# One PSUM input for the wide operations of a top-sixteen selection

## The reference, cut to what matters

```
q = (hf @ w_q).reshape(t, 8, 2, 64)
sc = einsum('thcd,hcnd->thcn', q, sub_keys)         # 2 x 128 scores a head and token
sv, si = top_k(sc, 16)
cand_s = (sv[:, :, 0, :, None] + sv[:, :, 1, None, :]).reshape(t, 8, 256)
cand_i = (si[:, :, 0, :, None] * 128 + si[:, :, 1, None, :]).reshape(t, 8, 256)
fs, fp = top_k(cand_s, 16)
eidx = take_along_axis(cand_i, fp, axis=-1)
gates = softmax(fs, axis=-1)
act = gelu(x . u_emb[eidx]);  out = sum over chosen of gates * act * v_emb[eidx]
```

## Time and profile before

| | us |
|---|---|
| median of 3 runs | 990.34 (989.86 to 990.83) |
| profiled run | 990.89 |
| its span | 989.0 |
| TensorE busy | 925.8 (94%) |
| VectorE busy | 734.6 (74%) |
| ScalarE busy | 529.0 (53%) |
| GpSimd busy | 464.1 (47%) |

### The profile page before, as it was taken

One profiled execution on the slowest core, in us unless ns is written; L12 is line 12 of the kernel. 1 busy time (PEld: TensorE's weight loads), 2 busy tenths in 40 slices (PEclk: granted clock), 3 DMA queues, 4 the chain that ended last, 5 costly groups with the idle time before them and its releaser, 6 DMA issues.

```text
span 989.0 us, 20056 instructions
## 1 busy us (share of the span) xinstructions
PE 925.8 (94%) x5888; PEld 828.0 (84%) x5888; DVE 734.6 (74%) x1591; ACT 529.0 (53%) x1042; POOL 464.1 (47%) x370
## 2 busy tenths in 40 slices
PE   7679399999979889999999999999999999999998
PEld 7546168899979889999999999988888888888886
DVE  5999944203999930388888888688888888888886
ACT  7333075555544445555555555665556666566653
POOL 4668406587999998877777777500000000000000
PEclk8789799999999999999999999999999999999999
DMA  9424022315556556656556556677767767776773
GB/s 341 155 86 155 16 85 75 118 55 202 197 186 210 183 199 215 210 198 202 196 189 205 191 190 202 202 252 237 250 237 243 241 237 245 235 245 238 246 240 134
DMA packets 67436, 191.39 MB, mean 194 GB/s; under 512 B 6480, under 2 KB 8272, under 8 KB 67408
## 3 DMA queue, kind: packets, MB, share of 16 engines
q1 hardware_dynamic: 67408, 191.04, 57.0%
HBM read 173.71 MB, written 17.30 MB: 193 GB/s over the span
## 4 chain that ended last, share of the span: by engine, by line
PE 66%; POOL 11%; DVE 10%; issue 8%; ACT 3%; DMA 1%; POOLq 0%; SPq 0%; DVEq 0%; ACTq 0%
PE ps L423 21%; PE ps L425 20%; PE ps L424 20%; POOL w_lo L1462 10%; DVE routing L731 4%; PE ps L660 3%; DVE routing L876 2%; DVE small L731 1%; PE ps L405 1%; DVE route_t L731 1%; DMA routing<-in_w_in 1%; DVE raw L731 1%; ACT w_hi L1168 1%; ACT h_hi L1175 0%; POOL w_lo L1426 0%
## 5 line engine op out<-in xcount | busy, mean ns | idle before, releaser
L1462 POOL TENSOR_TENSOR w_lo<-raw,w_hi 128x512 fp32r<-128x512 f32 x256 | 345.6, 1372 | 79.2 <-ACT w_hi L1318 78.8
L1318 ACT ACTIVATE w_hi<-raw 128x512 fp32r<-128x512 f32 x512 | 308.3, 628 | 132.2 <-PE ps L425 131.3
L423 PE MATMUL ps<-h_hi,w_hi 128*128 128x256 f32 x1088 | 309.6, 285 | 16.5 <-POOL w_lo L1462 15.2
L424 PE MATMUL ps<-h_lo,w_hi 128*128 128x256 f32 x1088 | 307.8, 283 | 0.0
L425 PE MATMUL ps<-h_hi,w_lo 128*128 128x256 f32 x1088 | 307.8, 283 | 0.0
L423 PEld LDWEIGHTS ps<-h_hi,w_hi 128*128 128x128 f32 x1088 | 208.7, 192 | 19.4 <-POOL w_lo L1462 17.4
L731 DVE TENSOR_TENSOR w_lo<-raw,w_hi 128x512 fp32r<-128x512 f32 x256 | 177.4, 693 | 52.5 <-ACT w_hi L1318 41.1
L424 PEld LDWEIGHTS ps<-h_lo,w_hi 128*128 128x128 f32 x1088 | 208.8, 192 | 0.0
L425 PEld LDWEIGHTS ps<-h_hi,w_lo 128*128 128x128 f32 x1088 | 208.8, 192 | 0.0
L423 PE MATMUL ps<-w_hi,hot_gate 128*128 128x512 f32 x512 | 199.2, 389 | 0.0
L424 PE MATMUL ps<-w_lo,hot_gate 128*128 128x512 f32 x512 | 199.2, 389 | 0.0
(11 more groups left out here) (195 smaller groups left out, 914.9 us busy)
## 6 DMA issues: line engine op xcount, KB each, us to landing
raw<-in_u_t SPq DMA_DIRECT2D x128, 512.0 KB, 3.3
raw<-in_v SPq DMA_DIRECT2D x128, 512.0 KB, 3.3
act_spill<-acts SPq DMA_DIRECT2D x62, 256.0 KB, 2.1
acts<-act_spill SPq DMA_DIRECT2D x62, 256.0 KB, 3.4
routing<-in_w_in SPq DMA_DIRECT2D x5, 2048.0 KB, 11.4
routing<-in_w_out SPq DMA_DIRECT2D x2, 2048.0 KB, 8.4
routing<-in_w_q SPq DMA_DIRECT2D x2, 2048.0 KB, 8.0
xs<-in_x SPq DMA_DIRECT2D x2, 512.0 KB, 4.0
```

What stands on the lines that cost most here:

```text
L423: pe.matmul(dst, s_hi, m_hi, start=first and i == 0, stop=False)
L424: pe.matmul(dst, s_hi, m_lo, start=False, stop=False)
L1318: A.activation(w_hi[:, 2 * (s % 2) + h, :], raw[:, s, h * HALF:(h + 1) * HALF], ACT.Copy)\
L1462: G.tensor_tensor(w_lo[:, slot, :], raw[:, s, h * HALF:(h + 1) * HALF], w_hi[:, slot, :].bitcast(F32), ALU.subtract).then_inc(lo_ready, 1)
```

## The change

Each of the wide operations with two inputs gets one of them from PSUM. The pair sum reads the second set's best values from best_p (bank 3), into which a new copy puts them. The compare reads iota_p (bank 2) in place of iota, and writes its result to match_p (banks 4 to 7) in place of w2; the product reads match_p. For this the iota copy and its two waits stand ahead of the selection instead of ahead of the one-hots, and a wait for all eight score copies (sc_ready at 8) stands ahead of the compares. Operation counts: two copies more, everything else as before. No engine but VectorE has a changed instruction.

```
+        best_p = ps[:, 3, 0:PH * PK].rearrange("p (h k) -> p h k", h=PH)
+        match_p = ps[:, 4:8, :].rearrange("p b n -> p (b n)").rearrange("p (h a b) -> p h a b", h=PH, a=PK)
...
-            iota_k = iota[:, 0:PK].unsqueeze(1).unsqueeze(1).to_broadcast(shape)
+            iota_k = iota_p[:, 0:PK].unsqueeze(1).unsqueeze(1).to_broadcast(shape)
+            dve.wait_ge(pq_ready, PH)
+            V.tensor_copy(iota_p, iota).then_inc(iota_ready, 1)
+            dve.wait_ge(iota_ready, 1)
             for t in range(TT):
                 dve.wait_ge(sc_ready, 4 * t + 4)
                 best([top[:, c, h, :] for c, h in ch_rows], [idx[:, c, h, :] for c, h in ch_rows],
                      [sc[:, t, c, h, :] for c, h in ch_rows], [work[:, c, h, :] for c, h in ch_rows])
                 did(V.tensor_copy(idx_f, idx))
-                step(tt(w2, top[:, 0].unsqueeze(3).to_broadcast(shape), top[:, 1].unsqueeze(2).to_broadcast(shape), ALU.add))
+                step(V.tensor_copy(best_p, top[:, 1]))
+                step(tt(w2, top[:, 0].unsqueeze(3).to_broadcast(shape), best_p.unsqueeze(2).to_broadcast(shape), ALU.add))
...
                 step(V.tensor_copy(ab_f, ab))
+                dve.wait_ge(sc_ready, 8)
                 for c in range(2):
-                    step(tt(w2, ab_f[:, c].unsqueeze(3).to_broadcast(shape), iota_k, ALU.is_equal))
-                    step(tt(w3, w2, idx_f[:, c].unsqueeze(2).to_broadcast(shape), ALU.mult))
+                    step(tt(match_p, ab_f[:, c].unsqueeze(3).to_broadcast(shape), iota_k, ALU.is_equal))
+                    step(tt(w3, match_p, idx_f[:, c].unsqueeze(2).to_broadcast(shape), ALU.mult))
...
-            dve.wait_ge(pq_ready, PH)
-            V.tensor_copy(iota_p, iota).then_inc(iota_ready, 1)
-            dve.wait_ge(iota_ready, 1)
             one_hots(0, first=True)
```

## The result

| | kernel before | changed kernel |
|---|---|---|
| median, us (runs) | 990.23 (4) | 974.19 (4) |
| lowest to highest | 989.86 to 990.83 | 973.15 to 975.58 |
| span of the profiled run | 989.0 | 971.9 |
| ratio, 95% interval | | 0.984 (0.982 to 0.986) |

The changed kernel is 16.0 us faster; 973.9 had been forecast, with a range of 972.6 to 977.0.

The account below looks back on a forecast made before the run. The prediction took TensorE to be held in the selection by GpSimd subtractions, which VectorE's wide operations with two SBUF inputs slow. Median 990.34 - 16.62 (loss) + 0.2 (small operations) = 973.9 us, range 972.6 to 977.0.

Parts of the forecast that it names:

- The size, 16.62 us: Key stage beside the selection: 28 tiles took 97.26 us instead of 80.64; the change gives back all 16.62 us.
- The ruler: ScalarE's gelu, one per tile of the key stage, used to size the loss: 2.88 us a tile when nothing is late.
- the view of waits: Profile view in which TensorE waited ten times, 14.0 us, always for the GpSimd subtraction w_lo.
- part 1: Selection's ten operations take one input from PSUM: GpSimd keeps its own pace, 2.55 us a tile, giving back 16.62 us.
- VectorE at 2.28 us an operation: Selection's ten 2048-element operations: 22.8 us instead of 32.0, 9.2 us less on VectorE, worth nothing by itself.
- parts 2, 3: Two best_p copies, 0.6 us on VectorE, hidden by idle time; iota copy moved ahead of the selection, costed at nothing.
- part 5: Selection's four compares write PSUM: between 0 and 9.7 us more on VectorE, taken as 0, either end inside idle time.
- part 6: Small SBUF operations of the selection still hold GpSimd: 0.2 us taken, bounds 0 and 2.7 us.
- The wait for the exponentials: VectorE's wait for ScalarE's exponentials after the selection: about 24 instead of 32.49 us.
- Partial release: Rival, chance 0.06: compares writing PSUM still hold GpSimd, sums and products let it go; 979.9 us.
- no release: Rival, chance 0.03: long instructions, not a second SBUF input, hold GpSimd; time stays at 990.3 us.
- Slower: Rival, chance 0.01: dear PSUM accesses make VectorE's selection late for ScalarE's exponentials; about 998 us at 7 us each.

Follow-up runs that it names:

- e3: Only the compares read PSUM (iota_p), and they write SBUF; sums and products read two SBUF tensors; 983.33 us, ratio 0.993 to the kernel before.

## Why the prediction was right

- *What bounds the stage.* Right. GpSimd set the pace beside the ten operations, in eight tiles of the selection (two of them held two operations each and lost 3.3 us), and TensorE in the tiles between; the changed kernel has all tiles at 2.88.
- *The size, 16.62 us.* Measured 16.61 between the first gelu and the exponentials. The ruler served better than the view of waits (14.0): it is what TensorE's work cost, without modelled ends.
- *GpSimd is let go by one PSUM input* (part 1). Right, and the step that carried the forecast. The rows for it were from another stage, with other forms and lengths; the separate kernels show it for sums, compares and products alone. The Trainium skill's rule in "SBUF — State Buffer", "Who interferes with whom", agrees in all of them: two SBUF inputs hold GpSimd (1.3 to 1.9 us of TensorE's time each), one doesn't, if the instruction is outside the two-port modes. Which mode the shift and the casts ran in that still waited with one input, no run here shows.
- *VectorE at 2.28 us an operation*: 2.29 to 2.30. The surcharge for a PSUM source that the Trainium skill has in "VectorE: DVE Perf Modes", section on the TRN2 errata (62 cycles, as an estimate 65 ns), didn't show: 2288 ns for the sums with a PSUM operand against 2286 for a reduce from SBUF and 2.28 us for a sum with both inputs in SBUF.
- *The copies* (parts 2, 3): 0.28 us each for best_p, 0.29 for iota_p, hidden by VectorE's idle time. Both waits were met. Without the reads they moved nothing.
- *Writing PSUM* (part 5): 2296 ns for a compare, 10 more than for the same compare with its output in SBUF (e3, 2286), as the 11 ns worked out for the copy had it. The low end of the bounds was the right one.
- *The small operations* (part 6) were the one term that I had taken above zero, 0.2 us. They lengthened a subtraction by 0.12 at most and cost no tile. The term was 0.0. With it at nothing the sum gives 990.34 - 16.62 = 973.7; that, not 973, is also the lower end of what the forecast alone allows. The 0.3 to 0.5 us between these sums and the measured median is no more than the front varies.
- *The wait for the exponentials*, forecast at about 24 us, measured 25.34: a cast (L1046 before, L1052 after) that had been held to 1.32 us took 0.30, so 1.0 us more was saved in the selection. It ended at 346.07, not 347.5; 0.56 of this is the shorter front.
- *Partial release and no release* are refuted, by the changed kernel itself and by the two kernels on input and output; length was put to the test by the quarters too. *Slower* was refuted for this change, not as a mechanism: 18 products more reached it.

What my working had not in it: the length of a holding operation decides who pays for it. For the kernel with quarters I had carried the 0.6 us of GpSimd's loss a quarter and nothing of VectorE's, and it came out at the expected time for another reason.

## What to carry to other kernels

When two engines each run slower together than alone, look for what the operations that hurt have in common, here two inputs in SBUF, and move one input of the engine with slack elsewhere; here copies of 0.3 us into PSUM, and an intermediate result kept there, freed 16 us of TensorE's time. Size such a loss by the distance between events that occur once a tile, and compare it with the stage's undisturbed distance: it held to 0.01 us here. Then look what the new idle time can carry: the exponentials fitted into it and gave 1.4 us more on the ruler.

## What the runs showed of the hardware that I had not expected

VectorE and GpSimd took turns here by whole instructions (the quarter that started at 286.33 us ended 0.55 us after the subtraction under way, as said under "Length"), so splitting the instructions of VectorE shifted the burden onto it. With VectorE's ten operations in quarters, GpSimd's subtraction took 1.62 us instead of 2.08 on the mean, and VectorE's work 61 us instead of 32.
